# Weight sums of a down projection: VectorE in the feed forward loop, or accumulating transfers from the attention stage on

## What is computed

```python
x = x + merged @ w_out
hf = rms(x, g_ffn)
x = x + (silu(hf @ w_gate) * (hf @ w_up)) @ w_down
return rms(x, g_final)
```

## Time and profile before

| What | Value |
|---|---|
| Time, median of 3 runs | 768.41 us (768.12 to 768.69) |
| Profiled execution, its own time | 768.33 us |
| Its span | 766.6 us |
| TensorE busy | 758.3 us, 99% |
| VectorE busy | 552.5 us, 72% |
| ScalarE busy | 355.4 us, 46% |
| POOL busy | 314.6 us, 41% |
| Bytes moved by DMA | 126.17 MB, mean 165 GB/s |

### The profile page before, as it was taken

One profiled execution on the slowest core, in us unless ns is written; L12 is line 12 of the kernel. 1 busy time (PEld: TensorE's weight loads), 2 busy tenths in 40 slices (PEclk: granted clock), 3 DMA queues, 4 the chain that ended last, 5 costly groups with the idle time before them and its releaser, 6 DMA issues.

```text
span 766.6 us, 9762 instructions
## 1 busy us (share of the span) xinstructions
PE 758.3 (99%) x3562; PEld 629.0 (82%) x3562; DVE 552.5 (72%) x752; ACT 355.4 (46%) x529; POOL 314.6 (41%) x169
## 2 busy tenths in 40 slices
PE   8999999999999999999999999999999999999997
PEld 7788887788888888888888888888888888888886
DVE  6999997684848484246767787777787677836687
ACT  6796567643535333634343423232323333434554
POOL 4456655233333333444444444444444354830000
PEclk9999999999999999999999999999999999999999
DMA  7744333022222443222233866666668567768853
GB/s 273 301 147 131 117 98 112 30 91 83 81 85 68 126 144 104 83 93 100 83 111 99 272 196 228 217 217 191 201 204 285 176 218 228 264 229 279 293 201 125
DMA packets 42371, 126.17 MB, mean 165 GB/s; under 512 B 4192, under 2 KB 6368, under 8 KB 40544
## 3 DMA queue, kind: packets, MB, share of 16 engines
q1 hardware_dynamic: 42192, 125.45, 49.1%
q10 hardware_dynamic: 144, 0.26, 0.1%
HBM read 107.08 MB, written 18.61 MB: 164 GB/s over the span
## 4 chain that ended last, share of the span: by engine, by line
PE 91%; ACT 3%; DVE 3%; DMA 1%; issue 1%; SPq 0%; POOL 0%; ACTq 0%
PE bank L1641 24%; PE bank L1643 24%; PE bank L1642 24%; PE bank L2005 4%; PE bank L2007 4%; PE bank L2006 4%; ACT uc L656 1%; DVE s5p L1015 1%; PE bank L1882 1%; PE bank L1757 1%; PE bank L1774 1%; DMA xT<-xt_dram 1%; ACT w_hi L596 1%; DVE tab_tmp L1015 1%; DVE h_lo L1020 1%
## 5 line engine op out<-in xcount | busy, mean ns | idle before, releaser
L535 POOL TENSOR_TENSOR w_lo<-raw,w_hi 128x1024 fp32r<-128x1024 f32 x90 | 218.1, 2424 | 300.7 <-ACT w_hi L596 300.7
L596 ACT ACTIVATE w_hi<-raw 128x1024 fp32r<-128x1024 f32 x112 | 118.8, 1060 | 310.9 <-PE bank L1643 306.3
L1641 PE MATMUL bank<-h_hi,w_hi 128*128 128x512 f32 x608 | 238.5, 392 | 0.2 <-POOL w_lo L540 0.2
L1643 PE MATMUL bank<-h_hi,w_lo 128*128 128x512 f32 x608 | 236.7, 389 | 0.0
L1642 PE MATMUL bank<-h_lo,w_hi 128*128 128x512 f32 x608 | 236.6, 389 | 0.0
L1641 PEld LDWEIGHTS bank<-h_hi,w_hi 128*128 128x128 f32 x608 | 114.2, 188 | 24.3 <-issue 1.0
L1643 PEld LDWEIGHTS bank<-h_hi,w_lo 128*128 128x128 f32 x608 | 114.1, 188 | 23.9
L1642 PEld LDWEIGHTS bank<-h_lo,w_hi 128*128 128x128 f32 x608 | 114.2, 188 | 23.7 <-issue 0.5
L540 POOL TENSOR_TENSOR w_lo<-raw,w_hi 128x512 fp32r<-128x512 f32 x48 | 67.2, 1420 | 52.4 <-ACT w_hi L596 46.0
L1015 DVE TENSOR_TENSOR mix<-mix 128x512 f32<-128x512 f32 x44 | 47.6, 1083 | 13.1 <-DMA mix<-w_dram 11.9
L1015 DVE TENSOR_TENSOR lo<-raw,hi 128x1536 fp32r<-128x1536 f32 (+1 forms) x19 | 32.8, 1732 | 24.8 <-ACT hi L925 24.6
(11 more groups left out here) (328 smaller groups left out, 1384.6 us busy)
## 6 DMA issues: line engine op xcount, KB each, us to landing
raw<-w_dram SPq DMA_DIRECT2D x112, 512.0 KB, 3.4
mix<-w_dram SPq DMA_DIRECT2D x11, 1024.0 KB, 8.0
mix_dram<-mix SPq DMA_DIRECT2D x11, 1024.0 KB, 6.3
raw<-w_dram SPq DMA_DIRECT2D x30, 256.0 KB, 4.3
raw<-mix_dram SPq DMA_DIRECT2D x26, 256.0 KB, 3.8
half_dram<-odd SPq DMA_DIRECT2D x11, 256.0 KB, 8.3
second<-half_dram SPq DMA_DIRECT2D x3, 768.0 KB, 6.0
raw<-mix_dram SPq DMA_DIRECT2D x3, 768.0 KB, 4.2
```

What stands on the lines that cost most here:

```text
L535: nc.gpsimd.tensor_tensor(w_lo[:, s, :], raw[:, s, :], fv(w_hi[:, s, :]), ALU.subtract).then_inc(w_ready, 1)
L596: nc.scalar.activation(w_hi[:, slot, :], raw[:, slot, :], ACT.Copy).then_inc(w_rounded, 1)
L1641: mm(out, a[0], b[0], start=first, stop=False)
L1643: return mm(out, a[1], b[0], start=False, stop=last)
```

## The change

The weights of the down projection become a tensor of their own, `down_dram`, in blocks of 128 x 512 that are contiguous in DRAM, and `mix_dram` takes the same layout. From tile 16 (T_MIX) on SP issues, behind the weight load of every tile up to 37, a copy of two blocks (512 KB) from `down_dram` to `mix_dram`, DRAM to DRAM, as 64 rows of 8 KB. Pair i's copies stand behind a wait until those of pair i - 1 have landed.

POOL then issues four accumulating transfers for each pair, 256 KB each, DRAM to DRAM: b12 += b11, b22 += b12 (of the original), then b11 += that, then b21 += that. They stand behind POOL's subtraction on every second tile: for pair i the first two at step 20 + 2i, the third at 22 + 2i, the fourth at 24 + 2i, where a step is the tile of the same number up to 22, and from 24 on the tile two later. Each waits for all earlier ones on its semaphore; the two of the first kind share one, so the second of them waits for the first to land. The loop of POOL is written out up to tile 61.

Out of the feed forward loop go the load of the pair, the four operations of VectorE and the store. As the transfers only add, the signs of the sums differ: two activation sums are formed with scalar_tensor_tensor, and the result sums of the right half subtract. The readers of the blocks read the new layout. Two semaphores are merged into one, and ScalarE has one wait less.

```diff
--- before.py
+++ after.py
@@ -46,8 +46,8 @@
 T_GLU = T_J2 + 4
 T_WO = T_J2 + 14
 T_FF = T_WO + KD
+T_MIX = T_VU
 T_DN = T_FF + 4 * (KF // 2)
-TILES = T_DN + KF
 PAIRS = KF // 2
 GROUPS = ((0, 2), (2, 5), (5, 8), (8, 11))
 UNITS = PAIRS + 2 * len(GROUPS)
...
@@ -358,6 +357,10 @@
             def leave(self, count):
                 assert self.n == self.per, self.n
                 self.base, self.n = self.outer + count * self.per, 0
+
+        def long_rows(blocks):
+
+            return blocks.rearrange("b p n -> (b p n)").rearrange("(r e) -> r e", e=2 * TILE)
 
         block = ctx.enter_context(nc.Block())
 
...
@@ -397,22 +400,22 @@
                 next_weights(t)
             sp.wait_ge(tok_sq, 4)
             sp.dma_start(sgu[:, :, :], sgu_d).then_inc(sgu_loaded, 16)
+            def copy_blocks(i, j):
+
+                if i:
+                    sp.wait_ge(mix_copied, 32 * i)
+                sp.dma_start(long_rows(mix_d[i, 2 * j:2 * j + 2]), long_rows(dn_d[2 * i + j]),
+                             max_dma_last_dim=8 * TILE).then_inc(mix_copied, 16)
+
             for t in range(8, T_WO):
                 next_weights(t)
+                if 0 <= t - T_MIX < 2 * PAIRS:
+                    copy_blocks(*divmod(t - T_MIX, 2))
                 if t == T_J2 - 2:
                     sp.wait_ge(ba_ready, ROUNDS)
                     sp.wait_ge(ca_ready, ROUNDS)
                     for i in range(len(X_PARTS)):
                         load_x(i)
-            def load_pair(i):
-                t = T_DN + 2 * i
-                sp.dma_start(mix[:, :, :].rearrange("p (a b) n -> p a (b n)", a=2),
-                             w_d[t:t + 2, :, :].rearrange("a p n -> p a n")).then_inc(mix_loaded, 16)
-
-            def store_mix(i):
-                sp.wait_ge(mixed, 4 * (i + 1))
-                sp.dma_start(mix_d[i, :, :], mix[:, :, :].rearrange("p a n -> p (a n)")).then_inc(mix_stored, 16)
-
             def store_half(i):
                 sp.wait_ge(ff_act, 2 * (i + 1))
                 sp.dma_start(half_d[i, :, :], odd[:, :]).then_inc(half_stored, 16)
...
@@ -437,31 +440,22 @@
                     sp.wait_ge(w_ready, T_DN - 1 + k)
                 elif k == 5:
                     sp.wait_ge(w_used, T_DN)
-                elif k == 6:
-                    sp.wait_ge(mix_stored, 16 * PAIRS)
                 elif k > 6:
                     unit_split(sp, {7: 0, 8: 1, 9: 2, 10: 6}[k])
-                sp.wait_ge(mix_stored, 16 * (k + 1))
                 slot, done = unit_raw[UNIT_SLOT[k]], unit_loaded[UNIT_SLOT[k]]
-                sp.dma_start(slot[:, 0:WB], w_d[T_DN + 2 * k, :, 0:WB]).then_inc(done, 16)
-                sp.dma_start(slot[:, WB:TILE], mix_d[k, :, WB:2 * WB]).then_inc(done, 16)
+                sp.dma_start(slot[:, 0:WB], dn_d[2 * k, 0]).then_inc(done, 16)
+                sp.dma_start(slot[:, WB:TILE], mix_d[k, 1]).then_inc(done, 16)
 
             for t in range(T_WO, T_DN):
                 next_weights(t)
                 i, j = divmod(t - T_FF, 4)
-                if i == 0 and j == 3:
-                    sp.wait_ge(x1_ready, 5)
-                    load_pair(0)
                 if i == 1 and j < 2:
                     store_x1(j)
-                if i > 0 and j == 2:
-                    store_mix(i - 1)
                 if i > 0 and j == 3:
-                    sp.wait_ge(mix_stored, 16 * i)
-                    load_pair(i)
                     store_half(i - 1)
                 if i == 8 and j == 0:
                     sp.wait_ge(x1_moved, 16 * 8)
+                    sp.wait_ge(mix_t4, 16 * PAIRS)
                     for k in (2, 3, 4):
                         load_unit(k)
 
...
@@ -471,16 +465,16 @@
                     sp.wait_ge(ready3, u - 2)
                 dst, done = raw3[u % 3], load3[u % 3]
                 if u < PAIRS:
-                    sp.dma_start(dst[:, 0, :], mix_d[u, :, 0:WB]).then_inc(done, 16)
-                    sp.dma_start(dst[:, 1, :], mix_d[u, :, 3 * WB:4 * WB]).then_inc(done, 16)
-                    sp.dma_start(dst[:, 2, :], w_d[T_DN + 2 * u + 1, :, WB:TILE]).then_inc(done, 16)
+                    sp.dma_start(dst[:, 0, :], mix_d[u, 0]).then_inc(done, 16)
+                    sp.dma_start(dst[:, 1, :], mix_d[u, 3]).then_inc(done, 16)
+                    sp.dma_start(dst[:, 2, :], dn_d[2 * u + 1, 1]).then_inc(done, 16)
                     return
                 k0, k1 = GROUPS[(u - PAIRS) % 4]
                 if u < PAIRS + 4:
                     for k in range(k0, k1):
-                        sp.dma_start(dst[:, k - k0, :], w_d[T_DN + 2 * k + 1, :, 0:WB]).then_inc(done, 16)
+                        sp.dma_start(dst[:, k - k0, :], dn_d[2 * k + 1, 0]).then_inc(done, 16)
                 else:
-                    sp.dma_start(dst[:, 0:k1 - k0, :], mix_d[k0:k1, :, 2 * WB:3 * WB].rearrange("k p n -> p k n")
+                    sp.dma_start(dst[:, 0:k1 - k0, :], mix_d[k0:k1, 2].rearrange("k p n -> p k n")
                                  ).then_inc(done, 16)
 
             def load_half(g):
...
@@ -490,7 +484,6 @@
 
             for k in range(2):
                 load_unit(k)
-            store_mix(PAIRS - 1)
             load_unit(5)
             store_half(PAIRS - 1)
             for k in range(6, 10):
...
@@ -545,6 +538,29 @@
                 for j, done in enumerate((w_half, w_ready)):
                     low_half(s, j).then_inc(done, 1)
 
+            def add(to, of, done, i):
+
+                if i:
+                    pool.wait_ge(done, 16 * i)
+                nc.gpsimd.dma_start(long_rows(to), long_rows(of), accum_op=ALU.add,
+                                    max_dma_last_dim=8 * TILE).then_inc(done, 16)
+
+            def weight_sums(t):
+
+                i = (t - T_MIX - 4) // 2
+                if (t - T_MIX) % 2 == 0 and 0 <= i < PAIRS:
+                    pool.wait_ge(mix_copied, 32 * (i + 1))
+                    add(mix_d[i, 1:2], dn_d[2 * i, 0:1], mix_b12, 2 * i)
+                    add(mix_d[i, 3:4], dn_d[2 * i, 1:2], mix_b12, 2 * i + 1)
+                i -= 1
+                if (t - T_MIX) % 2 == 0 and 0 <= i < PAIRS:
+                    pool.wait_ge(mix_b12, 16 * (2 * i + 2))
+                    add(mix_d[i, 0:1], mix_d[i, 3:4], mix_t2, i)
+                i -= 1
+                if (t - T_MIX) % 2 == 0 and 0 <= i < PAIRS:
+                    pool.wait_ge(mix_t2, 16 * (i + 1))
+                    add(mix_d[i, 2:3], mix_d[i, 0:1], mix_t4, i)
+
             for t in range(NS):
                 for j, done in enumerate((w_half, w_ready)):
                     pool.wait_ge(first_rounded, 2 * t + j + 1)
...
@@ -558,6 +574,7 @@
                                     fill=0.0, base=0, channel_multiplier=-1).then_inc(wst_masked, 1)
             for t in range(T_QK + 4, T_J1):
                 low_weights_in_halves(t % NS, t)
+                weight_sums(t)
             for t in range(T_J1, T_J1 + NS):
                 low_weights(t % NS, t)
             pool.wait_ge(uc_ready, 16)
...
@@ -572,7 +589,10 @@
             pool.wait_ge(sgu_taken, 4)
             nc.gpsimd.memset(toep[:, :, :], 0.0)
             nc.gpsimd.drain().then_inc(pads_ready, 1)
-            with nc.gpsimd.Fori(T_J1 // NS + 1, T_DN // NS) as i:
+            for t in range(T_J1 + NS, T_WO):
+                low_weights(t % NS, t)
+                weight_sums(t - NS)
+            with nc.gpsimd.Fori(T_WO // NS, T_DN // NS) as i:
                 for s in range(NS):
                     low_weights(s, i * NS + s)
 
...
@@ -942,7 +962,6 @@
             act.wait_ge(w_used, T_DN)
             round_three(0)
             act.wait_ge(ff_lo, PAIRS + 1)
-            act.wait_ge(mix_stored, 16 * PAIRS)
             act.wait_ge(half_stored, 16 * (PAIRS + 1))
             round_three(1)
             act.wait_ge(w_used, T_DN + PAIRS)
...
@@ -1470,21 +1489,12 @@
             even = parts[:, 0:2, :].rearrange("p a n -> p (a n)")
             a21, a11, s_1, s_2, s_3, s_4 = (parts[:, j, :] for j in range(6))
             a22, a12 = odd[:, 0:HALF], odd[:, HALF:T]
-            b11, b12, b21, b22 = (mix[:, j, :] for j in range(4))
             with nc.vector.Fori(0, PAIRS) as i:
                 for n in range(2):
                     dve.wait_ge(w_used, 4 * i + (T_FF + n + 1))
                     dve.wait_ge(ff_lo, i + 1)
                     tt(silu[:, n, :], bank[n][:, :], rstd[:, :], ALU.mult).then_inc(ff_g, 1)
 
-                dve.wait_ge(mix_loaded, 16 * i + 16)
-                tt(b22, b22, b12, ALU.subtract).then_inc(mixed, 1)
-                dve.wait_ge(mixed, 4 * i + 1)
-                tt(b12, b12, b11, ALU.subtract).then_inc(mixed, 1)
-                dve.wait_ge(mixed, 4 * i + 2)
-                tt(b11, b22, b11, ALU.add).then_inc(mixed, 1)
-                dve.wait_ge(mixed, 4 * i + 3)
-                tt(b21, b21, b11, ALU.subtract).then_inc(mixed, 1)
                 for n, hidden in enumerate((even, odd[:, :])):
```

(37 more changed lines are left out.)

3 lines of the change are left out of this document (1 added, 2 removed).

## The result

The changed kernel takes 790.42 us (median of 4 runs, 787.92 to 792.59) against 768.53 for the kernel before beside it: ratio 1.0284, 95% interval 1.027 to 1.0298, some 22 us slower. The profiled execution took 787.92 us with a span of 786.2, so its own loss is 19.6 us.

What follows compares the result with a forecast made beforehand. TensorE was taken as the bound, busy 99% of the span, with POOL closest to its path. Removed work, copies and sign changes counted zero; POOL's stalls of 12.0 us took 768.33 to 780.3, given as 780.4 us, range 768.0 to 801.

Steps and rivals of the forecast that it cites:

- the sum: POOL's added transfers: stalls of TensorE at tiles 20 to 42, block less gap at each, 12.0 us in all.
- What is removed is worth nothing: Feed forward loop: 47.6 us of VectorE work on mix, with its loads and stores, lies beside back-to-back matmuls; zero gain.
- The SP copies are hidden: SP's queue, tiles 16 to 37: 22 copies of 512 KB delay a weight load at most 3.4 us; taken as zero.
- Rival 3: Attention stage: copies make weight loads late, about 1.4 us each over tiles 19 to 24, +8, 788 us; chance 0.08.
- The sign changes and the new layout cost nothing: Same number and shapes of instructions, and down projection reloads of the same bytes in contiguous blocks: zero.
- POOL blocked by the first landing, with PE waiting for w_lo: Every second tile from 20 to 42, POOL waits for the first b12 add; the next tile's w_lo queues behind, stalling PE.
- The term L: Time from issue to landing of one 256 KB add on POOL: taken as 4.8 us, bounds 2.0 and 8.3.
- s: Time of each further transfer issue on POOL: taken as 0.9 us, bounds 0.44 and 1.42.
- block: How long POOL is held per event, L + n x s: 5.7 us at tile 20, 6.6 at 22, 7.5 at nine later tiles.
- Rival 2: Adds land late: an add counts twice as traffic, L goes to 8.3 us, about 40 us lost, 809 us; chance 0.13.
- The gaps: Time POOL may be blocked before PE waits: 3.96 us at tile 20, 5.49 at 22, then 4.76 to 9.17.
- Nothing by way of VectorE: The forecast counted only PE's waits for POOL's late w_lo, and no loss through VectorE.

Runs made afterwards that it cites:

- sums_out: Kernel before the change, with its weight sums left out (one VectorE operation on mix remains, on a single column; loads and stores of mix stay): 768.76 us, ratio 1.0003.
- next_later: Changed kernel with each pair's second b12 add moved behind the next tile's subtraction and copies and adds starting eight tiles later, shared semaphore kept: 768.57 us, ratio 0.9999.
- copies_only: Changed kernel without POOL's adds, so without the weight sums; the copies on SP's queue stay: 768.43 us, ratio 1.0005.
- own_sems: Changed kernel with a semaphore for each b12 add of a pair, so POOL no longer waits for the first to land: 768.88 us, ratio 1.0006.
- next_tile: Changed kernel with the second b12 add of each pair moved behind the next tile's subtraction; shared semaphore and all waits stay: 771.89 us, ratio 1.0048.
- plain: Changed kernel with POOL's 44 transfers moving their blocks without adding; issue, order, waits and bytes written stay: 776.8 us, ratio 1.0111.

## Why the prediction was right, and where it was off

The direction and the place were right, and the size was too small: 12 us forecast, 22 measured, within the range. Of these, 13.0 us of the profiled execution are TensorE's waits for w_lo, and that they lie so near the 12.0 of the sum is luck: two errors in it went in opposite directions, as told below.

- *What is removed is worth nothing*: right, by sums_out (1.0003), by the loop that keeps its 5.44 us a tile and, with the loads and stores of `mix` gone too, by next_later (0.9999).
- *The SP copies are hidden*: right, by copies_only. Rival 3 is out.
- *The sign changes and the new layout cost nothing*: right, by next_later, which has them all.
- *POOL blocked by the first landing, with PE waiting for w_lo*: right, by own_sems and next_tile.
- *The term L* was mis-sized: 4.8 us, measured 4.7 to 6.1 in the attention stage and at tile 26, and 6.1 to 8.0, mean 7.1, at the eight events from tile 28 on (6.5 counted from when POOL was free). s was nearly right, about 0.8 us by the ends of the rows for 0.9. From the end of a subtraction to the end of the last issue it is 9.1 us in the mean at the eight events, for a block of 7.5. In own_sems and next_tile, where POOL hardly stands still for it, the first landing is 5.2 us in the mean at the same events, near the forecast. Rival 2 (L 8.3, block 11.0) had the mechanism in part: adding does lengthen a landing, but by a third to a half and not to double, as the rule of the Trainium skill (Collectives: The Full Stack, The bandwidth ceiling) would have it for traffic between cores. The Trainium skill's fit (DMA: Bandwidth & Descriptors, Anatomy of one DMA) gives 2.6 us for 256 KB; the 3.6 that I took as L put the 1 us before the first byte on top of it. plain's 4.8 for the first landings and 3.0 for the second are nearer to that than 7.1, but no run had the queues to itself.
- *The gaps* were misread at some tiles. I took TensorE's start on tile t + 1 for the moment tile t ends, but between the tiles of a merge round it has 1.4 to 2.4 us of state space work. The real gaps are 6.8 at tile 26, 7.2 at 30, 36, 42 and 10.7 at 32, 38, with 6.4 at 28, 34, 40. So the stalls that I put largest (before tiles 31 and 43, 2.7 and 1.8 us) did not come, and tiles 29, 35 and 41 had them, with 3.1, 2.1 and 2.1 us of waiting. In the sum this error and the short L went in opposite directions: as an estimate from these gaps, the same sum gives some 5 us with the block of the forecast, and 13 to 14 with the measured blocks.
- *Nothing by way of VectorE*, for which the sum had no term: wrong in the attention stage. The forecast had 1.7 us there and 6.3 were lost: 3.9 by POOL, and 2.5 because VectorE, held up by POOL's subtractions, was late with what TensorE and ScalarE needed. The step that failed is that I asked only who waits for the late w_lo, and not whom POOL holds up when its work shifts. next_tile has this term nearly by itself, 3.4 us, and next_later, with no add in that stage, has none of it.
- *The clock* was not in the forecast: about 1.9 us in the profiled execution, of the 19.6. Its granted clock was 0.997 and it was the fastest of four; the slower three have 0.995 and 0.992, which goes the way of the 2.5 us between it and the median. That the clock is all of that difference I have not shown.

## What to carry to other kernels

A wait for a transfer that stands in an engine's program between two steps of the critical pipeline costs its whole landing time less the gap, at each place anew; before adding one, read the gap from when the consumer really starts, not from when its last tile ended. Here the wait was only an accident of two independent transfers sharing a semaphore: a semaphore each made the same transfers free (own_sems), and so did one step more between issue and wait, once no add stood in the attention stage (next_later). Read the slack of every engine stage by stage: VectorE was busy for 72% of the span, and for 28.9 of the 30 us from 90 to 120. And where one engine is busy without a gap, as TensorE is here from 60 to 740 us, work taken off another gained nothing.
